# The opening of a three-layer kernel in another order: modulation columns and x turned in two parts

## The reference

```python
cond = silu(c)                                    # c: 1024 values
mod = cond @ ada_w[i] + ada_b[i]                  # 1024 x 3072
shift, scale, gate = split(mod, 3)
h = rms_norm(x, norm_g[i]) * (1.0 + scale) + shift
proj = h @ w_in                                   # retention: 1024 x 6144
```

## Time and profile before

| | us |
|---|---|
| median of 3 runs | 2450.6 |
| lowest and highest | 2449.22, 2450.97 |
| the profiled execution, its own time | 2450.25 |
| span of the profiled execution | 2448.4 |
| TensorE busy in the span | 2419.0 (99%) |
| VectorE, ScalarE, GpSimd busy | 1578.4, 1105.7, 1235.7 |

### The profile page before, as it was taken

The page is one execution under the profiler, slowest core; times in us unless marked ns, Lnnn a source line. Parts: engine busy times, 40 slices in busy tenths (PEclk is TensorE's granted clock), DMA queues, the critical chain, the costliest instruction groups (busy, mean ns, idle before and its releaser), DMA issues.

```text
span 2448.4 us, 36045 instructions
## 1 busy us (share of the span) xinstructions
PE 2419.0 (99%) x13808; PEld 2076.6 (85%) x13808; DVE 1578.4 (64%) x2151; ACT 1105.7 (45%) x2052; POOL 1235.7 (50%) x883
## 2 busy tenths in 40 slices
PE   7999999999999999999999999999999999999999
PEld 6888898875588898899888899999988888788887
DVE  6965657588543386653766766666434489788863
ACT  5322223344544353322322226777534434888861
POOL 1645545430044455545555555555454445866664
PEclk9999999999999999999999999999999999999999
DMA  7554544493034345543332257454144343300034
GB/s 277 157 190 154 180 163 158 142 325 137 27 112 156 104 150 181 176 142 107 122 116 98 89 166 226 124 156 121 50 135 158 105 161 123 103 1 1 2 127 156
DMA packets 241196, 329.21 MB, mean 134 GB/s; under 512 B 19401, under 2 KB 173825, under 8 KB 239233
## 3 DMA queue, kind: packets, MB, share of 16 engines
q1 hardware_dynamic: 239552, 326.80, 40.3%
q10 hardware_dynamic: 1472, 0.10, 0.0%
HBM read 247.53 MB, written 79.33 MB: 133 GB/s over the span
## 4 chain that ended last, share of the span: by engine, by line
PE 91%; DVE 5%; issue 2%; ACT 1%; POOL 1%; DMA 1%; SPq 0%; DVEq 0%; ACTq 0%
PE ps L1182 23%; PE ps L1184 23%; PE ps L1183 23%; PE ps L1534 4%; PE ps L1707 2%; PE ps L1522 2%; PE ps L1688 2%; PE ps L1451 2%; PE ps L1470 2%; PE ps L1464 1%; DVE s_raw L2349 1%; PE ps L1375 1%; PE ps L1202 1%; PE ps L1434 1%; PE ps L1407 1%
## 5 line engine op out<-in xcount | busy, mean ns | idle before, releaser
L1068 POOL TENSOR_TENSOR w_lo<-raw,w_hi 128x512 fp32r<-128x512 f32 (+1 forms) x452 | 652.9, 1453 | 794.4 <-ACT w_hi L1813 758.8
L1813 ACT ACTIVATE w_hi<-raw 128x512 fp32r<-128x512 f32 (+1 forms) x456 | 282.9, 629 | 795.1 <-PE ps L1184 633.4
L1182 PE MATMUL ps<-w_hi,s_hi 128*128 128x256 f32 (+2 forms) x832 | 262.8, 316 | 0.8 <-POOL w_lo L1068 0.3
L1183 PE MATMUL ps<-w_lo,s_hi 128*128 128x256 f32 (+2 forms) x832 | 262.0, 315 | 0.0
L1184 PE MATMUL ps<-w_hi,s_lo 128*128 128x256 f32 (+2 forms) x832 | 262.0, 315 | 0.0
L1068 POOL TENSOR_TENSOR w_lo<-raw_wide,w_hi 128x512 fp32r<-128x512 f32 x112 | 174.0, 1560 | 131.3 <-ACT w_hi L1813 131.3
L2462 DVE TENSOR_TENSOR u<-u,ps 128x1024 f32<-128x1024 f32 (+1 forms) x96 | 116.4, 1212 | 148.9 <-PE ps L1184 145.5
L1182 PE MATMUL ps<-w_hi,a_hi 128*128 128x256 f32 (+2 forms) x624 | 196.7, 315 | 0.0
L1183 PE MATMUL ps<-w_lo,a_hi 128*128 128x256 f32 (+2 forms) x624 | 196.6, 315 | 0.0
L1184 PE MATMUL ps<-w_hi,a_lo 128*128 128x256 f32 (+2 forms) x624 | 196.5, 315 | 0.0
L1182 PE MATMUL ps<-s_hi,w_hi 128*128 128x512 f32 x480 | 188.6, 393 | 3.2 <-DVE s_lo L2336 2.3
(11 more groups left out here) (341 smaller groups left out, 6214.6 us busy)
## 6 DMA issues: line engine op xcount, KB each, us to landing
raw<-in_w SPq DMA_DIRECT2D x159, 512.0 KB, 4.3
ada_c<-in_ada SPq DMA_DIRECT2D x14, 2304.0 KB, 10.8
blk<-u SPq DMA_DIRECT2D x54, 512.0 KB, 4.0
raw_wide<-in_w SPq DMA_DIRECT2D x32, 512.0 KB, 4.6
blk<-c SPq DMA_DIRECT2D x27, 512.0 KB, 3.4
blk<-m1s SPq DMA_DIRECT2D x27, 512.0 KB, 3.3
ada_first<-in_ada SPq DMA_DIRECT2D x12, 768.0 KB, 16.0
r_g<-blk SPq DMA_DIRECT2D x8, 1024.0 KB, 9.4
```

What stands on the lines that cost most here:

```text
L1068: pool.tensor_tensor(w_ring(w_lo, n), w_source(n), w_ring(w_hi, n).bitcast(F32), ALU.subtract)\
L1182: pe.matmul(out, a_hi_, b_hi_, start=first, stop=False, skip_group_check=True)
L1183: pe.matmul(out, a_hi_, b_lo_, start=False, stop=False, skip_group_check=True)
L1813: act.activation(w_ring(w_hi, n), w_source(n), ACT.Copy).then_inc(w_rounded, 1)
```

## The change

Only the first layer's opening is rewritten. In words:

- **Loads.** The `ada` pieces come in the order 2, 0, then the first weights (R11 and the second block's first quarter), then 3, 1, then R21 and the second block's other quarter, and the lower half of x after them. Before: 1, 0, 2, 3 in one row, with weights and x after.
- **Pieces 2 and 0** are multiplied on TensorE in a new form, `first_rows`: `c_wide` holds each value of `ccol` 32 times over, a row group of `ada` is the moving operand, and the result (512 columns in 32 equal rows) goes to one of the four column groups of the array, n modulo 4. Nine matmuls make a piece. VectorE copies the bank to `acc_first`, and `first_columns` adds the four groups with a vector that is 1 in rows 0, 32, 64 and 96. Piece 1 has the same form, but stands in the middle of product (1,0). Piece 3 stays on VectorE, after the splits of a11.
- **Columns in two parts.** The first half (pieces 0 and 2, for k = 0 to 3) sets `cols_ready` to 1, the second (pieces 1 and 3, for k = 4 to 7) sets it to 2.
- **x in two parts.** k = 0 to 3 of the upper half are turned in the opening, 4 and 5 ahead of product (1,0), 6 and 7 ahead of (0,1). The lower half is turned in (1,1), no longer in (1,0) and ahead of (0,1).
- **ScalarE, VectorE.** a12 and the statistics of the lower half of x move from the opening into `first_block`, behind the copy of product (0,0). GpSimd no longer waits for `first_acc`.

```diff
-            for n in (1, 0, 2, 3):
+            def load_ada(n):
...
+            load_ada(2)
+            load_ada(0)
             load_raw(R11, 0)
             load_second(0, 0)
+            load_ada(3)
+            load_ada(1)
             load_raw(R21, 0)
+            load_second(0, 1)
             for b in range(4):
                 sp.dma_start(x_first[:, b], t["x"][(4 + b) * P:(5 + b) * P, :]).then_inc(x1_got[b], 16)
-            load_second(0, 1)
...
-            pool.wait_ge(first_acc, 3)
...
+            def first_rows(bank, piece, slices):
+
+                for n in slices:
+                    k, group = (6, 7, 8, 0, 1, 2, 3, 4, 5)[n], slice(32 * (n % 4), 32 * (n % 4) + 32)
+                    mm = pe.matmul(ps[group, bank, :], c_wide[:, k], ada_first[piece][:, k], start=(n < 4),
+                                   stop=(n >= 5), skip_group_check=True)
+                    if n == ADA - 1:
+                        mm.then_inc(cols_done, 1)
+
+            def first_columns(bank, piece):
+
+                pe.wait_ge(first_acc, (2, 4, 1, 3)[piece])
+                over = ones[:, 0:1] if piece == 3 else c_wide[:, ADA, 0:1]
+                for j in range(4):
+                    mm = pe.matmul(ps[:, bank, 4 * piece + j:4 * piece + j + 1], acc_first[:, piece, j * P:(j + 1) * P],
+                                   over, start=True, stop=True, skip_group_check=True)
+                if piece < 2:
+                    mm.then_inc(cols_done, 1)
...
+                if (s, i) == (1, 0):
+                    turn_half(0, 0, (4, 5))
+                if (s, i) == (0, 1):
+                    turned_evac(pe, 0, 0, 3)
+                    for piece in (3, 1):
+                        first_columns(7, piece)
+                    turn_half(0, 0, (6,))
+                    pe.wait_ge(cols_ready, 2)
+                    turn_half(0, 0, (7,))
...
-                        if (s, i, k) == (FIRST_BLOCK[l] + 1, 0, 1 if l else 2):
+                        if (s, i, k) == (1, 0, 2):
+                            turned_evac(pe, 0, 0, 2)
+                            pe.wait_ge(ada_second, 16 * 3)
+                            first_rows(6, 1, range(ADA))
+                        if (s, i, k) == ((FIRST_BLOCK[l] + 1, 0, 1) if l else (1, 1, 2)):
                             turn_half(l, 1, range(4, 8))
-                        if (s, i, k) == ((FIRST_BLOCK[l] + 1, 0, 3) if l else (0, 1, 0)):
+                        if (s, i, k) == ((FIRST_BLOCK[l] + 1, 0, 3) if l else (1, 1, 3)):
                             turn_half(l, 1, range(4))
...
+            for c in (2, 0, 1):
+                pe.wait_ge(ada_in[1][c], 16)
+                first_rows(0, 2, [3 * ((c + 1) % 3) + n for n in range(3)])
+            pe.wait_ge(ada_in[0][2], 16)
+            first_rows(1, 0, range(3))
+            turn_half(0, 0, range(4))
+            first_columns(2, 2)
+            for c in (0, 1):
+                pe.wait_ge(ada_in[0][c], 16)
+                first_rows(1, 0, [3 * (c + 1) + n for n in range(3)])
+            first_columns(2, 0)
             pe.wait_ge(cols_ready, 1)
...
+                else:
+                    m1s_copy(s)
+                    product_slots(s, 1)
+                    for k in (4, 6):
+                        turned(0, 0, k)
+                    for c in range(2):
+                        variant(0, "a12", c)
+                    for b in range(2):
+                        stats(0, 1, b)
+                    m1s_copy(s + 1)
+                    product_slots(s + 1, 1)
+                    for b in range(2, 4):
+                        stats(0, 1, b)
...
-            for k in (4, 6):
-                turned(0, 0, k)
-            for b in range(4):
-                stats(0, 1, b)
-            for c in range(2):
-                variant(0, "a12", c)
```

More of the change, by code:

```diff
@@ L2499, in first_block @@
                 s = FIRST_BLOCK[l]
[L2500 to L2504 removed]
+                if l == 0:
+                    for n in range(2):
+                        weight_sum(s, n)
+                for b in range(4):
+                    normalized(l, 1, b)
+                weight_sum(s, 2)
                 variant_low(l, "a22", 0)
@@ new lines, in first_columns @@
+            def first_columns(n, half, bank):
+                dve.wait_ge(cols_done, n)
+                part, at = slice(4 * half, 4 * half + 4), 4 * half
+                dve.tensor_copy(cols[:, 0, 0, part], ps[:, bank, at:at + 4])
+                dve.scalar_tensor_tensor(cols[:, 0, 1, part], ps[:, bank, KD + at:KD + at + 4], 1.0, norm_col[:, 0, part],
+                                         ALU.add, ALU.mult).then_inc(cols_ready, 1)
+                dve.wait_ge(cols_ready, half + 1)
+            first_rows(1, 0, 2)
```

105 lines of the change are left out of this document (42 added, 63 removed).

## The result

| | before | changed |
|---|---|---|
| median of 20 runs each, us | 2450.28 | 2454.0 |
| lowest and highest | 2449.22, 2451.08 | 2453.07, 2455.31 |
| span of the profiled execution | 2448.4 | 2453.1 |

The changed kernel takes 1.0016 times as long, with a 95% interval of 1.0009 to 1.0023: 3.7 us more, by the medians. That is 0.16%, inside the 0.2% that the prediction called "within", and its 2454.3 was 0.3 us off. The profiled execution of the changed kernel took 2454.84, 0.8 us over its median. Its first `ada` chunk also landed 0.8 us later (11.74) than in nine profiles of variants with the same opening (10.8 to 11.0), so its clock times are best read as distances from P, the first matmul of product (0,0).

A forecast was written before the change was run, and what follows sets the result against it. TensorE, 99% busy, was taken as the bound, with the ScalarE/VectorE chain deciding (0,3): 27.0 + 51.5 = 78.5, 3.7 us later; on 2450.25 that is 2454.0, plus 0.35 for the median, 2454.3. Range 2447 to 2460.

The forecast's parts named there:

- within: Outcome too close to no change for a measurement to tell: 0.2%, 4.9 us; given a chance of 0.49.
- clock lost in (0,1): Product (0,1), after TensorE's wait: ten matmuls at 0.43 us instead of 0.23 at the lower clock, 2.0 us.
- four sums and the split: VectorE ahead of (0,3): four sums of x and a split, 10.2 us with GpSimd working in the same stretch.
- the other side of the clock and GpSimd: Low end of the forecast: no clock lost at (0,1), -2.0 us, and sums free of GpSimd, -4.1 us.
- nothing given back behind (0,3): Up to about 100 us TensorE hangs on the same VectorE chain, so the 3.7 us delay stays.
- a second chain beside TensorE's own work: ScalarE and VectorE work from the second columns to the sums, putting (0,3) 3.7 us later; chance 0.60.
- TensorE's own work: TensorE's stream from the first product to (0,3): 34.0 us before, 6.4 added, 40.4; alone 7.4 us earlier.
- rival D: ScalarE and VectorE are looser than reckoned, so TensorE's stream decides up to (0,3): 7.4 us faster, 2443.2; chance 0.12.
- Rival B: The opening stays at 1.2 GHz, first product at 30 to 32.9 us: 6.7 to 9.6 slower, 2457 to 2460; chance 0.20.
- Rival C: Column groups don't run side by side with 512 columns, delaying opening and piece 1: 17.2 us slower, 2467.8; chance 0.08.
- a GpSimd or VectorE one: TensorE's wait at (0,2) for a GpSimd or VectorE split, expected in the profile; no size given.
- The 11 us of waits: Part of the 51.5 us from the first product to (0,3) in which TensorE waits, 11 us.

## Why the prediction was right

By its own steps, in distances from P:

| step | predicted | measured |
|---|---|---|
| P, first chunk at 10.9 | 27.0 | 26.8 to 27.2 (variants); 27.72, first chunk at 11.74 |
| piece 1's nine matmuls | 2.8 | 2.7 (39.16 to 41.85) |
| (0,1); wait ahead of it | P + 23.3; 3.4 | P + 23.1; 3.1 |
| clock lost in (0,1) | 2.0 | 2.1 |
| lower x transposed | P + 33.6 | P + 33.9 |
| first sum | 68 to 69 us | 69.07 (P + 41.35) |
| four sums and the split | 10.2 | 10.1 |
| (0,3) | P + 51.5 | P + 51.6 |
| what the other side of the clock and GpSimd would give | -2.0 and -4.1 | -1.7 and -3.4, the latter with the clock of (0,2) in it |
| nothing given back behind (0,3) | 3.7 | 3.7 (medians); in the profile 4.5 at (0,3), 4.7 at the end, with P 0.7 late |

- **The decisive choice** was to reckon a second chain beside TensorE's own work. TensorE's own work alone gave a gain of 7.4 us (rival D), and P 13 us earlier looks like 13 us gained. The chain from the second columns over a12, statistics, a22 and sums gave a loss, and that is what came.
- **Rival B** falls: the weight loads of the transposes are short at once.

```profile
L1205 PEld LDWEIGHTS ps<-ident,xn x16: 137/141/143, 18.6 to 20.2; 128*128 128x128 f32 x16
```

 They took 230 ns at 1.2 GHz. The clock rose while only the matmuls with 32 columns of weights ran: the first twelve records took 3.58 us, and from 15.60 on six take 1.06. The 15 us of one-column matmuls before hadn't. On the rule of the Trainium skill that the prediction weighed ("TensorE: Matmul & The Clock Gate", Part 4, PE-mode transpose), this run can't decide, as the clock was up before the transposes began.
- **Rival C** falls for the changed kernel, and its size was right: the kernel with one group.
- **Rival D** falls: the waits of 3.1 and 3.3 us are there.
- **Not in the sum:** the wait for GpSimd at (0,2) was named as "a GpSimd or VectorE one", without a size. It is 3.3 us, and the clock is at 1.2 GHz behind it: (0,2) takes 7.34 us up to the wait at (0,3), and 5.56 in the kernel with GpSimd out of the way (70.39 to 75.95), so 1.8 us are lost. It added nothing here, since VectorE's sums were later still, by 0.32 us at (0,3). That the two chains end so close together is luck for the sum: with a half clock as long as in the variant with piece 1 earlier, where (0,2) took 8.40 us, (0,3) would have come some 0.7 us later (an estimate, 8.40 - 7.34 - 0.32). The kernel with the weights of (0,2) earlier showed how near it stood to the path: take it away, and most of it comes back at (0,3). The 11 us of waits that the prediction counted from P + 40.4 to P + 51.5 are these: 3.12 + 3.29 + 0.32 of waiting and 2.1 + 1.8 of half clock, 10.6 in all. TensorE's own work was thus 41.0 us, not 40.4.
- **The clock behind the wait at (0,1)** was taken at its full price from one earlier place, and that reading had a slip: between the column sums and P TensorE was not idle throughout, it did eight transposes from 39.16 on. The half clock came in all three kernels with this wait in place and nothing in it (the changed one, one group, GpSimd shortened). Other waits of this case, at the end of this text, show that the length of a wait alone doesn't tell it.
- **Piece 3** on VectorE took 8.2 us (30.36 to 38.56), not 6.2: part of it ran beside GpSimd's splits of the second block's weights. It ended 0.6 us ahead of piece 1's matmuls (39.16), so the slip cost nothing.
- **The later blocks** have the waits that they had, for the reason that the prediction gave: TensorE still waits for VectorE there (2.4 us in all from 80 to 130 us, mostly for splits of the sums; 2.3 before, from 75 on), and VectorE's sums were as late as (0,3). Where they were in time, in the variant with piece 1 earlier, some 0.8 us came back.

## What to carry to other kernels

Moving the first product earlier is worth only what the second chain allows: follow every engine's work from the moved point to the place where it last met the old schedule, and count there. Work that lay under the opening's DMAs was free; in the stream it costs its own time, and what is handed to the other engines later because of it costs more. A short wait of TensorE can have a second price, the half clock after it, and a wait that is removed often only shows the one behind it, so ask which engine would have been late anyway before giving a figure.

## What the runs showed of the hardware

- **A wait and the clock.** Every wait of 3.07 to 3.30 us in these profiles was followed by a granted clock of 0.50, for 3 to 6 us. It cost 2.1 us in (0,1) and 1.8 in (0,2) of the changed kernel, and 2.8 in (0,2) of the variant with piece 1 earlier (8.40 against 5.56 us). Behind shorter waits it went either way: 1.00 behind 2.27 us (GpSimd shortened) and behind 2.80 us at (0,3) (the chain of the lower x pulled forward), 0.50 behind 1.82 us at (0,3) (sums in another order) and within 2 us behind 2.92 (weights of (0,2) earlier). So the length of the wait alone doesn't decide. The first row is of the variant with piece 1 earlier, behind its wait of 3.29 us, the second of the chain pulled forward, behind 2.80 us:

```profile
68.00:70.00 2.00, 2.00 (x6) 1.52 (x5) 1.97 (x2) 0.59 (x1) 2.00 (x2) 0.50 0.19 17
...
74.00:76.00 2.00, 1.95 (x9) 1.65 (x10) 1.97 (x2) 0.93 (x1) 0.00 (x0) 1.00 0.00 0
```

- **The time at which the clock comes back** varies between executions of like streams. Behind the wait of 2.71 us that ends at P, the transposes of k = 4 and 5 start 7.2 us later in three profiles (34.14 - 26.98 in the kernel with the weights of (0,2) earlier) and 7.6 to 8.3 us later in the others. This alone is a spread of 1.1 us in kernels whose gains are of that size.
- **Column groups with long right sides.** Nine fp32 matmuls of 32 x 512 take 2.76 us in four groups and 7.91 in one, 2.9 times as long.
- **VectorE beside GpSimd.** A subtraction of 128 x 1024 takes 1.22 us alone and 2.2 to 2.3 beside GpSimd, and scaling by a column 0.75 and 1.58 (53.05 and 56.96 above). GpSimd's split took 1.5 us each in one place (3.04 for two from 61.14, in the kernel with the weights of (0,2) earlier) and 2.2 in another (4.42 for two from 66.67). GpSimd's splits cut short were worth 3.4 us, nearly the whole loss of the change, with the clock that stayed up in (0,2) included.
